# Window attention in two layers: masks and sinks laid down first in the scores' PSUM banks, one mask product per head, sinks as float32r products of three parts

## The chip, the cores and the metric

One core of one Trainium2 chip runs the whole program. The metric is the device time in microseconds of that core, from launch to end. A profiled execution has its own time, and a span from its first to its last instruction.

## The reference, cut to what matters

Two transformer blocks follow one another on 512 latent tokens and 256 context tokens of width 1024. The first block has full attention (a low-rank kind and a grouped kind), an mLSTM mixer and two feed-forward layers. The second block has two layers, each with windowed attention, a Fourier mixer, a short convolution and a gated merge. Only the windowed attention is changed:

```python
BLOCK = WINDOW = 128; 8 heads of 64, 2 key/value heads
def sink_softmax(s, sink_b):
    m = jnp.maximum(jnp.max(s, axis=-1, keepdims=True), sink_b)
    e = jnp.exp(s - m)
    return e / (jnp.sum(e, axis=-1, keepdims=True) + jnp.exp(sink_b - m))

# for each block of 128 latent queries (start = i * BLOCK):
valid = (jnp.abs(qpos[:, None] - kpos[None, :]) <= WINDOW) & (kpos >= 0) & (kpos < n)
s_loc = jnp.where(valid, einsum('bqkgd,bnkd->bkgqn', qi, ks), -jnp.inf)
s_ctx = einsum('bqkgd,bnkd->bkgqn', qi, kc)          # all 256 context tokens
p = sink_softmax(concatenate([s_ctx, s_loc]), sink_b)
o = p[..., :nc] @ vc + p[..., nc:] @ vs
# context queries (layer 0 alone): the 256 context keys, the same sink softmax
```

A block of 128 latent queries sees the context (two tiles of 128 keys), its own tile, and its left and right neighbour where there is one; the neighbours are masked along a diagonal.

## The kernel before, in words

Everything is laid out with features on partitions. Five engine programs are written out by hand; each engine runs its own list in order, and waits are semaphores with named steps (`step("s", w, p, s)` and the like). `plan()` lists the phases; here the phases `("attn", "win0")` and `("attn", "win1")` matter, each between the layer's projection jobs and its Fourier mixer.

`attn_pairs` lists the pairs of a stage. A pair is one tile of 128 queries (`qt`) and two heads, `s` = 0 and 1, one of each key/value head. Layer 0 has 24 pairs (two context tiles, four latent tiles, times four `j`), layer 1 has 16. A pair has `L` columns of scores: 256 for a context tile, 512 for the first and the last latent tile, 640 for the two in the middle. One more column, at `L`, holds the sink, so `wide` is `L + 1`. Head `s` writes its scores in the two PSUM banks `pairs[s]`.

On TensorE, `scores(p)` waits until the exponentials of pair `p - 1` have been read out of both heads' banks. For each piece of columns it issues one float32 product per head, head 0 in the upper 64 rows of the array and head 1 in the lower 64 (a float32 product is two instructions in the trace). Pieces are cut at column 512 and at the edges of masked tiles. Behind a piece with a masked tile it adds the mask by a float32r product of the identity with the mask (`BAND`), one for each masked tile and head; at the end comes a float32 product of one row of ones and the sink. Step `("s", w, p, s, 0)` is given when 512 columns are complete, `("s", w, p, s)` after the sink. Then `turn(u)` transposes the previous pair's probabilities, and `pv` multiplies them by the values, one half of a block of two pairs behind each pair.

On VectorE, `negmax` takes the maximum of the first 512 columns, then of the rest (the sink among it), and combines them; `evict` copies a quarter of the transposes; `scale` divides by the sum. On ScalarE, `exps` takes the exponential of `wide` columns with its sum, and `evict` copies the other three quarters. The order on ScalarE is: the previous pair's first eviction, both exponentials, the two other evictions. On VectorE it is: both heads' maxima, one eviction, both scalings.

Before the first scores of a stage, VectorE writes `BAND` (identity and two masks, two casts, lines 1812 and 1813) and TensorE waits for step `("band", w)`. These casts stand in VectorE's list behind its last product of the projection jobs (`Y`, line 1633). `BAND` lies in the space of the scratch row `T[5]`.

In the trace a score product is line 1069, a mask line 1073, a sink line 1077, a transpose line 1120, a value product line 1133; VectorE's maxima are lines 1821 and 1823 (line 1828 for 256 columns), the combination line 1825 (1830), its eviction 1839, its scaling 1846 and 1848; ScalarE's exponential is line 1448 and its eviction 1458.

Of the kernel before, what the change touches and what calls it, by code (L numbers as in the profile page):

```python
# [16 lines left out]
F32 = mybir.dt.float32  # L17
# [273 lines left out]
def build_program(nc, dram, step):  # L291
# [73 lines left out]
    BAND = sb("BAND", [P, 3, P], 188, F32R)  # L365
# [49 lines left out]
    def attn_pairs(which):  # L415

        pairs_of = []

        def pair(**kw):
            kw["b"], kw["r"] = len(pairs_of) // 2, len(pairs_of) % 2  # L420
            kw["nt"] = kw["L"] // P
            kw["wide"] = kw["L"] + (kw["sink"] is not None)
            pairs_of.append(kw)

        if which == "even":
            for hp in range(HEADS // 2):
                for qt in range(6):
                    L = CTX if qt < 2 else TOK
                    pair(q=[MQ[:, 2 * hp + s, qt * P:qt * P + P] for s in range(2)], L=L, masks=[], sink=None, split=False,
                         k=[(0, [MK[:, 2 * hp + s, 0:L] for s in range(2)])], out=(hp, qt),  # L430
                         v=[[VM[:, i, (2 * hp + s) * 64:(2 * hp + s) * 64 + 64] for i in range(L // P)] for s in range(2)])
            for qt in range(6):
                L = CTX if qt < 2 else TOK
                for j in range(4):
                    pair(q=[GQ[64 * s:64 * s + 64, j, qt * P:qt * P + P] for s in range(2)], L=L, masks=[], sink=None, split=True,
                         k=[(0, [GK[64 * s:64 * s + 64, 0, 0:L] for s in range(2)])], out=(j, qt),
                         v=[[VG[:, i, 64 * s:64 * s + 64] for i in range(L // P)] for s in range(2)])
        else:
            l = int(which[3])
            t0 = 0 if l == 0 else CTX  # L440
            for qt in range(t0 // P, 6):
                near = [i for i in (qt - 1, qt, qt + 1) if 2 <= i < 6] if qt >= 2 else []
                masks = [(CTX + n * P, 1 if i < qt else 2) for n, i in enumerate(near) if i != qt]
                tiles = [0, 1] + near
                ks = [(0, [SK[64 * s:64 * s + 64, 0, 0:CTX] for s in range(2)])]
                if near:
                    ks.append((CTX, [SK[64 * s:64 * s + 64, 0, near[0] * P:near[-1] * P + P] for s in range(2)]))
                for j in range(4):
                    c = PARAMS["sink"] + l * HEADS + j
                    sinks = [PAR[0:1, c + 4 * s:c + 4 * s + 1] for s in range(2)]  # L450
                    pair(q=[SQT[64 * s:64 * s + 64, j, qt * P - t0:qt * P - t0 + P] for s in range(2)], k=ks, L=len(tiles) * P,
                         masks=masks, sink=sinks, split=True, out=(j, qt),
                         v=[[SV[:, i, 64 * s:64 * s + 64] for i in tiles] for s in range(2)])
        return pairs_of
# [456 lines left out]
    def _(eng):  # L911
# [73 lines left out]
        for p in phases:  # L985
# [59 lines left out]
            elif p[0] == "attn":  # L1045
# [9 lines left out]
                def scores(p):  # L1055
                    x = prs[p]
                    pieces = []
                    for c0, k in x["k"]:
                        n = k[0].shape[-1]

                        edges = {512 - c0} | {e - c0 for m in x["masks"] for e in (m[0], m[0] + P)}
                        cuts = sorted(c for c in edges if 0 < c < n)
                        for a, b in zip([0] + cuts, cuts + [n]):
                            pieces.append((c0 + a, c0 + b, [t[:, a:b] for t in k]))
                    last = [None, None]

                    def piece(s, a, b, k, ms):
                        pos = (64 * s, 0) if x["split"] else (0, 0)
                        last[s] = mm(pairs[s][:, a:b], x["q"][s], k[s], start=True, stop=not ms, tile_position=pos)  # L1069

                    def mask(s, ms):
                        for c, m in ms:
                            last[s] = mm(pairs[s][:, c:c + P], BAND[:, 0, :], BAND[:, m, :], start=False, stop=True)

                    def sink(s):
                        if x["sink"] is not None:
                            last[s] = mm(pairs[s][:, x["L"]:x["wide"]], ONES[0:1, :], x["sink"][s], start=True, stop=True)
# [9 lines left out]
                    if x["split"]:  # L1087
                        free_scores(0)
                        free_scores(1)
                        for a, b, k in pieces:  # L1090
                            ms = [m for m in x["masks"] if a <= m[0] < b]
                            piece(0, a, b, k, ms)
                            piece(1, a, b, k, ms)
                            for s in range(2):
                                mask(s, ms)
                                if x["wide"] > 512:
                                    first_bank(s, b)
                        for s in range(2):
                            sink(s)
                            last[s].then_inc(*pe.mark("s", w, p, s))  # L1100
                    else:
                        for s in range(2):
                            free_scores(s)
                            for a, b, k in pieces:
                                piece(s, a, b, k, [])
# [434 lines left out]
    def _(eng):  # L1540
# [169 lines left out]
        for pi, p in enumerate(phases):  # L1710
# [429 lines left out]
```

## Time and profile before

| | us |
|---|---|
| median of 3 runs | 2902.92 |
| lowest and highest | 2902.10, 2913.47 |
| the profiled execution | 2902.85 |
| its span, first to last instruction | 2901.0 |
| TensorE busy (products) | 2635.5 |
| VectorE busy | 1297.1 |
| ScalarE busy | 932.1 |
| mean granted TensorE clock | 0.946 of full |

The busy times are over the whole program; the ends of products are modelled, so a busy TensorE is not one at its peak. A granted clock of 1.00 is 2.4 GHz, 0.50 is 1.2 GHz. The window attention stages lie at 2330 to 2443 us (layer 0) and 2725 to 2817 us (layer 1) of the span.

### The profile page before, as it was taken

What the parts mean: (1) busy time and instruction counts of PE and PEld (TensorE: products, weight loads), DVE (VectorE), ACT (ScalarE), POOL (GpSimd) and SP (SyncE); (2) the same over time, 40 slices, a digit from 0 to 9 for tenths busy, and PEclk for the clock granted to TensorE, in tenths of its full rate; (3) what the DMA queues carried; (4) which work ended last, traced back from release to release, by engine and by line L of the source; (5) the groups of instructions that cost most, each with busy time, mean ns of one, the idle gap of its engine ahead of it and who ended that gap; (6) DMA issues with size and microseconds to landing.
All of it is one profiled execution on the core that took longest, in us unless ns stands there. A gap on an engine that the chain in (4) does not pass through costs nothing.

```text
span 2901.0 us, 35381 instructions
## 1 busy us (share of the span) xinstructions
PE 2635.5 (91%) x14496; PEld 2032.7 (70%) x14496; DVE 1297.1 (45%) x2324; ACT 932.1 (32%) x1619; POOL 173.3 (6%) x134
## 2 busy tenths in 40 slices
PE   4988799997999999989998989999979989949997
PEld 2765555585888888867876667777858866828765
DVE  3235378835333333354435453334452264373463
ACT  3234355623212122234233332222332143332342
POOL 0000001001101011010000010101100001000010
PEclk9999889997999999998999899999979999969898
DMA  5123300011343332211120135553211210102201
GB/s 213 64 70 92 119 13 1 1 44 59 114 132 110 123 118 68 68 55 59 59 73 1 30 121 169 167 171 127 88 55 62 60 54 1 54 23 84 98 1 58
DMA packets 66001, 223.20 MB, mean 77 GB/s; under 512 B 7216, under 2 KB 10928, under 8 KB 65072
## 3 DMA queue, kind: packets, MB, share of 16 engines
q1 hardware_dynamic: 63648, 214.13, 22.9%
q10 hardware_dynamic: 2192, 6.82, 0.6%
q8 instruction: 114, 1.87, 0.3%
q14 instruction: 47, 0.39, 0.0%
HBM read 218.82 MB, written 2.10 MB: 76 GB/s over the span
## 4 chain that ended last, share of the span: by engine, by line
PE 82%; DVE 10%; ACT 4%; DMA 2%; issue 1%; POOL 0%; SPq 0%; DVEq 0%; ACTq 0%
PE pair L959 21%; PE pair L961 20%; PE pair L960 20%; PE pair L1069 4%; DVE T L1790 3%; PE side L934 2%; PE side L1133 2%; PE pair L982 2%; ACT T L1448 2%; PE pair L1120 1%; DMA RAW<-in_w 1%; PE pair L1002 1%; DVE HL L1782 1%; PE pair L653 1%; PE pair L652 1%
## 5 line engine op out<-in xcount | busy, mean ns | idle before, releaser
L959 PE MATMUL pair<-HH,WH 128*128 128x512 f32 (+1 forms) x2432 | 886.5, 365 | 70.2 <-DVE HL L1782 67.5
L961 PE MATMUL pair<-HH,WL 128*128 128x512 f32 (+1 forms) x2432 | 865.6, 356 | 0.0
L960 PE MATMUL pair<-HL,WH 128*128 128x512 f32 (+1 forms) x2432 | 865.3, 356 | 0.0
L959 PEld LDWEIGHTS pair<-HH,WH 128*128 128x128 f32 x2432 | 465.3, 191 | 192.8 <-DVE HL L1782 87.9
L1558 DVE TENSOR_TENSOR WL<-RAW,WH 128x1024 fp32r<-128x1024 f32 (+4 forms) x286 | 320.7, 1121 | 513.0 <-ACT WH L1224 500.4
L961 PEld LDWEIGHTS pair<-HH,WL 128*128 128x128 f32 x2432 | 466.6, 192 | 65.8
L960 PEld LDWEIGHTS pair<-HL,WH 128*128 128x128 f32 x2432 | 467.3, 192 | 62.1 <-issue 2.6
L1224 ACT CAST WH<-RAW 128x1024 fp32r<-128x1024 f32 (+4 forms) x286 | 270.3, 945 | 548.9 <-DMA RAW<-in_w 531.6
L959 PE MATMUL pair<-DH,WH 128*128 128x512 f32 (+3 forms) x624 | 232.8, 373 | 8.4 <-POOL DL L1977 4.3
L960 PE MATMUL pair<-DL,WH 128*128 128x512 f32 (+3 forms) x624 | 223.6, 358 | 0.0
L961 PE MATMUL pair<-DH,WL 128*128 128x512 f32 (+3 forms) x624 | 223.1, 358 | 0.0
L1608 DVE SCALAR_TENSOR_TENSOR X<-pair,MOD,X 128x256 f32<-128x256 f32 (+1 forms) x120 | 79.4, 662 | 175.5 <-PE pair L961 172.6
L959 PEld LDWEIGHTS pair<-DH,WH 128*128 128x128 f32 (+1 forms) x624 | 119.8, 192 | 44.0 <-issue 9.9
L1448 ACT ACTIVATE T<-pair,STAT 128x768 f32<-128x768 f32 (+4 forms) x176 | 126.7, 726 | 18.6 <-DVE STAT L1830 12.0
L960 PEld LDWEIGHTS pair<-DL,WH 128*128 128x128 f32 (+1 forms) x624 | 119.7, 192 | 17.7
L961 PEld LDWEIGHTS pair<-DH,WL 128*128 128x128 f32 (+1 forms) x624 | 119.3, 191 | 18.2
L1572 DVE SCALAR_TENSOR_TENSOR T<-pair,PAR,T 128x255 f32<-128x255 f32 (+1 forms) x78 | 51.5, 661 | 170.4 <-ACT T L1283 144.4
L982 PE MATMUL pair<-T,CONST 96*96 96x512 f32 (+3 forms) x112 | 56.0, 632 | 73.1 <-DVE T L1652 45.3
L934 PE MATMUL side<-RAW,CVP 128*32 128x256 f32 x1152 | 96.9, 419 | 27.1 <-DVE CVP L1566 20.3
L1821 DVE TENSOR_REDUCE STAT<-pair 128x1 f32<-128x512 f32 x128 | 87.8, 686 | 49.5 <-PE pair L1069 38.3
L1283 ACT ACTIVATE T<-pair,PAR 128x768 f32<-128x768 f32 (+1 forms) x44 | 39.0, 886 | 191.2 <-PE pair L961 191.2
L1120 PE MATMUL pair<-CONST,T 128*128 128x128 f32 x506 | 92.8, 293 | 4.5 <-DVE T L1848 1.6
(278 smaller groups left out, 2754.1 us busy)
## 6 DMA issues: line engine op xcount, KB each, us to landing
RAW<-in_w SPq DMA_DIRECT2D x345, 512.0 KB, 3.6
RAW<-in_w SPq DMA_DIRECT2D x49, 384.0 KB, 3.1
RAW<-in_w SPq DMA_DIRECT2D x16, 256.0 KB, 2.7
DFL<-in_dft_lat ACTq DMA_DIRECT2D x4, 1024.0 KB, 7.7
X<-in_x SPq DMA_DIRECT2D x1, 3072.0 KB, 16.4
out_x<-X SPq DMA_DIRECT2D x8, 256.0 KB, 2.0
RAW<-in_w SPq DMA_DIRECT2D x12, 128.0 KB, 2.0
RAW<-in_w SPq DMA_DIRECT2D x8, 144.0 KB, 2.1
```

The costliest lines, as they stand in the source:

```text
L934: ins = mm(strip, CVP[:, round * 4 + k, :], RAW[:, s, k * j.m:(k + 1) * j.m], start=round == 0, stop=round == 1, tile_position=(0, 32 * k))
L959: mm(out[0:j.m, c:e], wh[k], a, start=k == 0, stop=False)
L960: mm(out[0:j.m, c:e], wh[k], b, start=False, stop=False)
L961: ins = mm(out[0:j.m, c:e], wl[k], a, start=False, stop=k == j.k - 1)
L982: ins = mm(pairs[2][0:rows, c:e], ones[0:rows, 0:rows], sq[0:rows, c:e], start=True, stop=True)
L1069: last[s] = mm(pairs[s][:, a:b], x["q"][s], k[s], start=True, stop=not ms, tile_position=pos)
L1120: ins = nc.tensor.transpose(attn_turned(c)[:, (i - a) * P:(i - a) * P + P], T[2 * (p % 2) + s][:, i * P:i * P + P], IDENT)
L1224: nc.scalar.copy(WH[:, j.n % NRING, 0:c], RAW[:, j.n % NRING, 0:c]).then_inc(*act.mark("hi", j.n))
L1448: A(T[2 * (p % 2) + s][:, 0:x["wide"]], pairs[s][:, 0:x["wide"]], AF.Exp, bias=STAT[:, st + 2 + s:st + 3 + s], accum_out=STAT[:, st + 6 + ...
L1558: TT(WL[:, j.n % NRING, 0:c], RAW[:, j.n % NRING, 0:c], WH[:, j.n % NRING, 0:c].bitcast(F32), ALU.subtract).then_inc(*dve.mark("lo", j.n))
L1790: STT(t[:, a:b], X[:, k, t0 + a:t0 + b], AB[:, s, k:k + 1], T[3][:, a:b], ALU.mult, ALU.mult).then_inc(*dve.mark("nmul", q["id"], k))
L1821: V.tensor_reduce(m[0], pairs[s][:, 0:512], AX, ALU.max).then_inc(*dve.mark())
```

## The change

- The score columns are reordered: the masked neighbours stand first, side by side, then the two context tiles, then the query's own tile. The neighbours of a middle tile are not adjacent in the keys, so one product reads both with a stride. The values' tiles follow the same order.
- One mask product per head covers both neighbours (256 columns for the middle tiles, 128 for the first and last latent tile) and is issued as the first product of the bank; the scores accumulate on it. The pieces are no longer cut at mask edges: three pieces for 640 columns instead of four, three for 512 columns as before.
- The sink is a float32r product of two columns with the full 128 rows, issued right after the mask, before the scores. Its operands are a matrix of ones and a matrix `SINKR[:, 3]`, whose rows 0, 1 and 2 hold the sink's three float32r parts and whose other rows are zero. It writes columns `L` and `L + 1`; only `L` is read.
- For 512 columns the step after the sink is the same as the step of the first 512 columns, for both heads.
- The two heads' score products follow each other with no mask between them.
- VectorE prepares the ones and the three parts in ten more operations before the first scores of each stage.

```diff
-    BAND = sb("BAND", [P, 3, P], 188, F32R)
+    BAND = sb("BAND", [P, 4, P], 188, F32R)
+    SINKR = sb("SINKR", [P, 4, 2 * HEADS + 2], 190, F32R)
+    SINKF = sb("SINKF", [P, 4, 2 * HEADS + 2], 190.5)
...
-                near = [i for i in (qt - 1, qt, qt + 1) if 2 <= i < 6] if qt >= 2 else []
-                masks = [(CTX + n * P, 1 if i < qt else 2) for n, i in enumerate(near) if i != qt]
-                tiles = [0, 1] + near
-                ks = [(0, [SK[64 * s:64 * s + 64, 0, 0:CTX] for s in range(2)])]
-                if near:
-                    ks.append((CTX, [SK[64 * s:64 * s + 64, 0, near[0] * P:near[-1] * P + P] for s in range(2)]))
+                beside = [i for i in (qt - 1, qt + 1) if 2 <= i < 6] if qt >= 2 else []
+                own = [qt] if qt >= 2 else []
+                tiles = beside + [0, 1] + own
+                n = len(beside) * P
+                ks, mask = [], None
+                if own:
+                    first = [1 if i < qt else 2 for i in beside]
+                    mask = BAND[:, first[0]:first[-1] + 1, :]
+                    ks.append((0, n, [SK[64 * s:64 * s + 64, 0, beside[0] * P:beside[-1] * P + P].rearrange("p (t x) -> p t x", x=P)[:, 0::2, :] for s in range(2)]))
+                ks.append((n, CTX, [SK[64 * s:64 * s + 64, 0, 0:CTX] for s in range(2)]))
+                if own:
+                    ks.append((n + CTX, P, [SK[64 * s:64 * s + 64, 0, qt * P:qt * P + P] for s in range(2)]))
...
-                        for a, b, k in pieces:
-                            ms = [m for m in x["masks"] if a <= m[0] < b]
-                            piece(0, a, b, k, ms)
-                            piece(1, a, b, k, ms)
+                        for s in range(2):
+                            if x["mask"] is not None:
+                                mm(pairs[s][:, 0:pieces[0][1]], BAND[:, 0, :], x["mask"], start=True, stop=False)
+                            if x["sink"] is not None:
+                                mm(pairs[s][:, x["L"]:x["L"] + 2], BAND[:, 3, :], x["sink"][s], start=True, stop=True)
+                        for n, (a, b, k) in enumerate(pieces):
                             for s in range(2):
-                                mask(s, ms)
+                                piece(s, a, b, k, n == 0 and x["mask"] is not None)
                                 if x["wide"] > 512:
                                     first_bank(s, b)
+                                    if x["L"] == 512:
+                                        pe.also("s", w, p, s)
                         for s in range(2):
-                            sink(s)
-                            last[s].then_inc(*pe.mark("s", w, p, s))
+                            if b > 512 or x["wide"] <= 512:
+                                last[s].then_inc(*pe.mark("s", w, p, s))
...
                     V.tensor_copy(BAND[:, 0, :], IDENT).then_inc(*dve.mark())
-                    V.tensor_copy(BAND[:, 1:3, :], CONST[:, 5:7, :]).then_inc(*dve.mark("band", w))
+                    V.tensor_copy(BAND[:, 1:3, :], CONST[:, 5:7, :]).then_inc(*dve.mark())
+                    V.tensor_copy(BAND[:, 3, :], ONES).then_inc(*dve.mark())
+                    c = PARAMS["sink"]
+                    left = PAR[:, c:c + 2 * HEADS]
+                    for n in range(2):
+                        V.tensor_copy(SINKR[:, n, 0:2 * HEADS], left).then_inc(*dve.mark())
+                        dve.wait_ge(*dve.own())
+                        TT(SINKF[:, n, 0:2 * HEADS], left, SINKR[:, n, 0:2 * HEADS].bitcast(F32), ALU.subtract).then_inc(*dve.mark())
+                        left = SINKF[:, n, 0:2 * HEADS]
+                        if n == 0:
+                            TS(SINKF[:, 2, 0:2 * HEADS], SINKR[:, 0, 0:2 * HEADS].bitcast(F32), IDENT[:, 0:1], None, ALU.mult).then_inc(*dve.mark())
+                        dve.wait_ge(*dve.own())
+                    STT(SINKF[:, 3, 0:2 * HEADS], SINKR[:, 1, 0:2 * HEADS].bitcast(F32), IDENT[:, 1:2], SINKF[:, 2, 0:2 * HEADS], ALU.mult, ALU.add).then_inc(*dve.mark())
+                    dve.wait_ge(*dve.own())
+                    V.memset(SINKF[:, 3, 2 * HEADS:2 * HEADS + 2], 0.0).then_inc(*dve.mark())
+                    STT(SINKR[:, 3, 0:2 * HEADS], SINKF[:, 1, 0:2 * HEADS], IDENT[:, 2:3], SINKF[:, 3, 0:2 * HEADS], ALU.mult, ALU.add).then_inc(*dve.mark())
+                    dve.wait_ge(*dve.own())
+                    V.tensor_copy(SINKR[:, 3, 2 * HEADS:2 * HEADS + 2], SINKF[:, 3, 2 * HEADS:2 * HEADS + 2]).then_inc(*dve.mark("band", w))
```

The first block's attention calls the same `scores` with no mask and no sink; its instructions stay the same.

## Rows read from the trace of the kernel before

**Rows 1.** The page, part 4: the chain that ended last, by engine.

```profile
PE 82%; DVE 10%; ACT 4%; DMA 2%; issue 1%; POOL 0%; SPq 0%; DVEq 0%; ACTq 0%
```

**Rows 2.** Windows: from:to, length, busy us of each engine, granted clock, DMA.

```profile
2332.70:2346.40 13.70, 12.39 (x45) 7.25 (x45) 7.29 (x30) 4.68 (x23) 0.00 (x0) 0.50 0.44 183
2348.67:2357.44 8.77, 7.86 (x48) 4.47 (x49) 7.20 (x30) 4.76 (x23) 0.00 (x0) 1.00 0.00 0
2357.44:2374.72 17.28, 15.46 (x121) 11.24 (x121) 13.72 (x47) 8.67 (x29) 0.00 (x0) 1.00 0.01 2
2374.72:2419.34 44.62, 43.36 (x349) 31.97 (x347) 33.08 (x94) 21.45 (x58) 0.00 (x0) 1.00 0.00 1
2419.34:2433.59 14.25, 14.06 (x110) 9.99 (x109) 10.30 (x34) 7.17 (x22) 0.00 (x0) 1.00 0.01 1
2725.30:2749.10 23.80, 20.66 (x101) 17.12 (x100) 14.13 (x43) 8.38 (x25) 0.00 (x0) 0.50 0.35 132
```

**Rows 3.** The chain in time, two pairs of 640 columns: start, us, engine and line.

```profile
2385.59 0.92 PE pair L1069 x8
2386.51 0.37 PE pair L1073 x2
2386.88 0.65 PE pair L1069 x8
...
2387.89 0.53 PE pair L1077 x4
...
2388.94 0.49 ACT PTW L1458
...
2391.13 0.92 PE pair L1069 x8
...
2395.46 1.45 PE side L1133 x12
```

**Rows 4.** The timeline of the first of these pairs, VectorE and ScalarE.

```profile
2387.33 0.69 DVE L1821 TENSOR_REDUCE STAT<-pair 128x1 f32<-128x512 f32 x1 [1.10 <-PE pair L1069]
2388.24 0.29 DVE L1823 TENSOR_REDUCE STAT<-pair 128x1 f32<-128x129 f32 x1 [0.21 <-PE pair L1077]
...
2388.70 0.68 DVE L1821 TENSOR_REDUCE STAT<-pair 128x1 f32<-128x512 f32 x1
2389.30 0.28 DVE L1823 TENSOR_REDUCE STAT<-pair 128x1 f32<-128x129 f32 x1
...
2389.61 0.21 DVE L1825 TENSOR_SCALAR STAT<-STAT 128x1 f32<-128x1 f32 x1
...
2390.10 0.80 ACT L1448 ACTIVATE T<-pair,STAT 128x641 f32<-128x641 f32 x1
```

**Rows 5.** The timeline of VectorE, pairs of 512 columns (first tile, last tile).

```profile
2367.52 0.69 DVE L1821 TENSOR_REDUCE STAT<-pair 128x1 f32<-128x512 f32 x1 [0.87 <-PE pair L1073]
...
2369.04 0.15 DVE L1823 TENSOR_REDUCE STAT<-pair 128x1 f32<-128x1 f32 x1
2369.22 0.21 DVE L1825 TENSOR_SCALAR STAT<-STAT 128x1 f32<-128x1 f32 x1
...
2425.82 0.69 DVE L1821 TENSOR_REDUCE STAT<-pair 128x1 f32<-128x512 f32 x1 [0.84 <-PE pair L1069]
```

**Rows 6.** The chain in time, the scores of the same two pairs.

```profile
2366.08 1.15 PE pair L1069 x12
...
2424.09 0.90 PE pair L1069 x8
```

**Rows 7.** The timeline of VectorE, its last cast before the stage in layer 0.

```profile
2329.59 0.29 DVE L1813 CAST BAND<-CONST 128x256 fp32r<-128x256 f32 x1
```

**Rows 8.** Windows in the first block's grouped attention, columns as in rows 2.

```profile
480.50:503.20 22.70, 18.05 (x118) 9.20 (x116) 19.04 (x63) 13.32 (x51) 10.48 (x8) 1.00 0.00 1
503.20:510.00 6.80, 6.36 (x21) 2.75 (x21) 4.13 (x14) 2.52 (x12) 0.00 (x0) 0.50 0.00 0
518.90:585.00 66.10, 62.70 (x433) 38.54 (x435) 60.26 (x158) 45.19 (x103) 0.00 (x0) 1.00 0.00 1
```

More of the change, by code:

```diff
@@ L428, in attn_pairs @@
                     L = CTX if qt < 2 else TOK
-                    pair(q=[MQ[:, 2 * hp + s, qt * P:qt * P + P] for s in range(2)], L=L, masks=[], sink=None, split=False,
-                         k=[(0, [MK[:, 2 * hp + s, 0:L] for s in range(2)])], out=(hp, qt),
+                    pair(q=[MQ[:, 2 * hp + s, qt * P:qt * P + P] for s in range(2)], L=L, mask=None, sink=None, split=False,
+                         k=[(0, L, [MK[:, 2 * hp + s, 0:L] for s in range(2)])], out=(hp, qt),
                          v=[[VM[:, i, (2 * hp + s) * 64:(2 * hp + s) * 64 + 64] for i in range(L // P)] for s in range(2)])
@@ L434, in attn_pairs @@
                 for j in range(4):
-                    pair(q=[GQ[64 * s:64 * s + 64, j, qt * P:qt * P + P] for s in range(2)], L=L, masks=[], sink=None, split=True,
-                         k=[(0, [GK[64 * s:64 * s + 64, 0, 0:L] for s in range(2)])], out=(j, qt),
+                    pair(q=[GQ[64 * s:64 * s + 64, j, qt * P:qt * P + P] for s in range(2)], L=L, mask=None, sink=None, split=True,
+                         k=[(0, L, [GK[64 * s:64 * s + 64, 0, 0:L] for s in range(2)])], out=(j, qt),
                          v=[[VG[:, i, 64 * s:64 * s + 64] for i in range(L // P)] for s in range(2)])
@@ L441, in attn_pairs @@
             for qt in range(t0 // P, 6):
[L442 to L447 removed]
+                beside = [i for i in (qt - 1, qt + 1) if 2 <= i < 6] if qt >= 2 else []
[10 more added lines that the diff above has]
+                    ks.append((n + CTX, P, [SK[64 * s:64 * s + 64, 0, qt * P:qt * P + P] for s in range(2)]))
                 for j in range(4):
[L449 to L450 removed]
+                    c = l * HEADS + j
+                    sinks = [SINKR[:, 3, c + 4 * s:c + 4 * s + 2] for s in range(2)]
                     pair(q=[SQT[64 * s:64 * s + 64, j, qt * P - t0:qt * P - t0 + P] for s in range(2)], k=ks, L=len(tiles) * P,
[L452 removed]
+                         mask=mask, sink=sinks, split=True, out=(j, qt),
                          v=[[SV[:, i, 64 * s:64 * s + 64] for i in tiles] for s in range(2)])
@@ L1057, in scores, with piece @@
                     pieces = []
[L1058 to L1064, printed above, removed]
+                    for c0, n, k in x["k"]:
+                        for a, b in ((c0, min(512, c0 + n)), (max(512, c0), c0 + n)):
+                            if a < b:
+                                whole = b - a == n
+                                pieces.append((a, b, k if whole else [t[:, a - c0:b - c0] for t in k]))
                     last = [None, None]
-                    def piece(s, a, b, k, ms):
+                    def piece(s, a, b, k, masked):
                         pos = (64 * s, 0) if x["split"] else (0, 0)
[L1069 to L1077, printed above, removed]
+                        last[s] = mm(pairs[s][:, a:b], x["q"][s], k[s], start=not masked, stop=True, tile_position=pos)
                     def first_bank(s, b):
```

2 lines of the change are left out of this document (1 added, 1 removed).

## The prediction

> **What bounds the kernel now.** I read the page first for its shares and its chain of waits: the chain that ended last lies 82% on TensorE and 10% on VectorE [rows 1], so a product taken out of the chain can shorten the kernel. The change touches only the two window attention stages. Their stretches are in [rows 2]; one pair of heads is a period there, and a period repeats within 0.02 us. In the first layer: eight pairs of 256 columns (three of them 8.77 us), four pairs of 512 columns for the first latent query tile (17.28 us, 4.32 each), eight periods of 640 columns (44.62 us), then 14.25 us for three periods of 512 columns of the last tile (4.75 each). The second layer has no 256 columns, spends 23.80 us at a granted clock of 0.50 (1.2 GHz) on its first pairs, and then repeats the 44.62 and the 14.25 us. In the first layer the 0.50 lasted 13.70 us.
>
> The chain in a pair of 640 columns [rows 3] is: scores and masks 0.92 + 0.37 + 0.65 + 0.37 us, sinks 0.53, transposes, ScalarE's eviction at 3.35 (2388.94 - 2385.59), exponentials, and the next scores at 5.54 (2391.13). So on the face of it TensorE's scores set the period. The queue order says why: ScalarE's exponentials of the next pair stand behind the eviction of this one, which waits for TensorE's transposes, which stand behind the scores. But VectorE's maxima run beside it [rows 4]: first maximum at 1.74 after the first product, second at 2.65 (it waited 0.21 us for the sink), head 1's first at 3.11, its second 0.60 later, its last small operation at 4.02, done with its release at 4.26. ScalarE began head 1's exponential at 4.51. VectorE's path is only 0.25 us behind the bound. That is the number on which the forecast turns.
>
> **The change, part by part.**
>
> (a) *TensorE's group in a pair of 640 columns.* Before: 0.92 + 0.37 + 0.65 + 0.37 + 0.53 = 2.84 us for 24 products. After: per head one mask of 256 columns and one sink lead, then 12 instead of 16 score products. The trace has no such leading block. The two first products are priced as the mask pair with its switch back to half-height products, 0.37 [rows 3], the two others as sink steps of 0.11 (four sinks with a switch behind them took 0.53), so 0.59. Bounds: 0.44 if all four are 0.11, 0.74 if they are twice 0.37. The scores: 512 columns took 1.15 us in one run of products [rows 6], four products of 128 columns add 0.22 (the 0.65 holds eight of them and a switch near 0.2), so 1.37. Sum 1.96, a saving of 0.88 us in each of 16 pairs. In those of the pairs that hold twelve value products (1.45 us, [rows 3]) TensorE itself was the bound, with a period of 5.71; there it drops out as well.
>
> (b) *What is late next.* The first maximum needs 512 columns of scores, now behind the whole leading block: 0.59 + 1.15 = 1.74, where it was 1.74. It does not come earlier at all. What goes is the wait for the sink: second maximum at 1.74 + 0.60 = 2.34, head 1's first 0.46 later at 2.80, its second 3.40, the last small operation 3.71, released 0.24 later at 3.95 (steps from [rows 4]). ScalarE's path would allow 4.51 - 0.88 = 3.63, so VectorE is the bound. From head 1's exponential to the next scores it is 5.54 - 4.51 = 1.03, so the period becomes 4.98. The TensorE path of a pair with twelve value products: 1.96, the same eviction, transposes and value products as before less 0.88, 5.78 - 0.88 = 4.90, just under it. So 16 x 4.98 = 79.7 against 2 x 44.62 = 89.2: **-9.5 us**.
>
> (c) *512 columns, first latent tile.* Here the mask stood last and the first maximum could start at 1.44 (2367.52 - 2366.08, [rows 5, 6]). After, it waits for the leading block: 0.59 + 1.15 + 0.04 = 1.78. VectorE was already the path there: head 1's second maximum, of one column, began at 2.96, its small operation 0.18 later [rows 5], released 0.24 later at 3.38, without a wait behind the first maximum. So everything moves by the difference, +0.31 to 0.34, and TensorE's 0.33 us that are saved behind it gain nothing. Four pairs in layer 0: **+1.3 us**.
>
> (d) *512 columns, last tile.* The mask stood in the middle, the first maximum at 1.73 (2425.82 - 2424.09, [rows 5, 6]), now 1.76 to 1.78. The period becomes that of (c), 4.64; three were 14.25, now 13.92; two layers: **-0.7 us**.
>
> (e) *256 columns.* Two sinks lead instead of four that follow; 0.37 + the same four products; the maxima waited before for the first sink, now for the scores. Within 0.05 each, +0.2 for all eight. The second layer's three slow pairs of 512 columns: the leading block costs VectorE about 0.6 at the half clock, TensorE saves about as much; the pair with value products, which TensorE binds, gains 0.5. **-0.2 us** for (e) together.
>
> (f) *The preparation on VectorE.* Ten operations more: one of 128 columns, nine of 2 to 16, in front of TensorE's first scores, which wait for the last of them. Nothing hides it: TensorE stood idle since its last product and VectorE had only just ended its product for Y. Before, the second cast's row lasted 0.29 [rows 7]. A small dependent step is 0.18 (2369.22 - 2369.04, [rows 5]); seven such, 0.14 for the 128 columns, two near 0.1 that wait for nothing, and 0.06: 1.6 us. Bounds: ten times 0.07 and ten times 0.21 (the small operation's own duration, [rows 4]), so 0.7 to 2.1. Two layers: **+3.2 us**. The initial wait of ScalarE's first exponential moves with it; its four transfers of Fourier tables are issued before and needed only after the stage.
>
> (g) *Clock.* Taken as unchanged, 0.
>
> Sum: -9.5 + 1.3 - 0.7 - 0.2 + 3.2 = -5.9 us. The profiled execution took 2902.85 us (span 2901.0 and 1.85 around it), which is 0.07 from the median of 2902.92. The stage ends go through to the kernel's end, since the Fourier products follow on the same engine. Forecast **2897.0 us**.
>
> **A rule of the Trainium skill against it.** The row first: in the first block's grouped attention, TensorE was busy for 18.05 of 22.70 us in pairs of 256 columns, and then the granted clock was 0.50 for the next 6.8 us; in pairs of 768 columns it was busy 62.70 of 66.10 and the clock stayed at 1.00 [rows 8]. The Trainium skill, "TensorE: Matmul & The Clock Gate", section "A second HAM failure mode: psum-queue depth-cycling", says that an engine which pauses briefly but often between groups of matmuls swings between its two clocks. By that rule the thinner groups after the change would cost time; the trace agrees for 256 columns and disagrees for 768. What it would cost here is worked out from rows in C and D.
>
> **The rivals.**
>
> *A. The forecast* (VectorE's maxima become the path). For it: 4.26 against 4.51 today. Chance 0.57; by its own bounds (leading block +-0.15 on some 30 pairs is +-4.5, preparation -1.8 to +1.0) 2891 to 2903.
>
> *B. TensorE's saving counts in full*, because the first maximum comes earlier than worked out (the leading products' weights load while TensorE waits for the exponentials). 16 x 0.88 = 14.1, for 12 pairs of 512 columns about 0.4 each, 4.8, less 3.2: 2887. Against it: the leading block must then cost VectorE nothing. Chance 0.06.
>
> *C. The clock is regained late.* Both stages begin at 0.50, and the first layer returns to 1.00 in pairs of 256 columns, which lose four of sixteen products. If it stays down to the pairs of 512 columns, two pairs of 512 columns lose about 2.3 each (23.80 us held some three and a half periods of the second layer, 6.7 each, against 4.32; [rows 2]) and four of half the columns about half of that: +9, so 2906. For it: [rows 8]. Against it: in the second layer the first pairs with value products brought it back. Chance 0.18.
>
> *D. The other side: the clock falls in the pairs of 640 columns.* TensorE's 1.96 + 0.5 before ScalarE's eviction would double, +2.4 on each; all 16: +38, so 2935. With nine pairs or more it is slower than before by over 0.5%, and from three pairs on no longer faster. Against it: after the change TensorE works about 4.4 to 4.9 of 4.98 us there, near the 0.95 of the pairs of 768 columns. Chance 0.05.
>
> *E. The change hardly acts*: another path (ScalarE's exponentials, VectorE's scaling of head 1) takes over at once, or the leading block is 0.74 and more. The period goes to 5.3 only: -4 in (b), +1.3 + 3.2: 2903. Chance 0.14.
>
> **How the numbers follow.** The likeliest is A, 2897.0. A change of 0.5% is 14.5 us, about what a measurement of this kernel can tell from none: one of the three runs of before lay at 2913.47. The range holds A, C and E and leaves B and D out: 2889 to 2908. Faster by over 0.5% (below 2888.4) needs B: 0.05. Slower by over 0.5% (above 2917.4) needs D or a later clock in both stages: 0.05. The rest, 0.90, is within 0.5%.
>
> **What would show it.** Pairs of 640 columns at a period of 4.98 with the first maximum still near 1.74 and its successor no longer waiting; the chain there through VectorE's maxima; the first latent tile's pairs at 4.6 instead of 4.32; 1.6 us more between VectorE's product for Y and TensorE's first scores; recorded score products down from 480 to 416 (a float32 product is two records), sinks from 160 to 80, masks from 96 to 64. Wrong would be: a first maximum that moves by more than 0.15, a clock of 0.50 inside the 640 columns, or a leading block far from 0.59.

## The result and the profile after

The changed kernel takes 2887.23 us (median of 18 runs, 2883.76 to 2895.39), the kernel before 2902.43 in the same comparison (18 runs, 2891.37 to 2913.99). The ratio is 0.9947, 95% interval 0.9934 to 0.9959: 15.2 us less, between 12 and 19. The forecast was 2897.0, some 6 less, in a range of 2889 to 2908. So the direction was right, and the size was not: the time lies 1.8 us below the range.

The profiled execution of after took 2895.39 us, the slowest of its 18, so its distance to the profile of before (2902.85) is 7.5 us. One execution is not the median here, and much of what follows is about that. (Over all profiled executions of the study the five of before have a mean of 2900.8 us and the three of after 2894.6, 6.2 less.)

Windows of after, to be laid beside [rows 2] (from:to, length, busy TensorE, weight loads, VectorE, ScalarE, GpSimd, granted clock, DMA):

```profile
2372.17:2381.29 9.12, 7.39 (x61) 5.22 (x61) 6.95 (x24) 4.98 (x15) 0.00 (x0) 1.00 0.00 1
2381.29:2420.72 39.43, 35.87 (x282) 25.81 (x283) 31.24 (x93) 22.85 (x57) 0.00 (x0) 1.00 0.01 1
2420.72:2434.40 13.68, 12.38 (x102) 8.78 (x103) 10.33 (x35) 7.80 (x22) 0.00 (x0) 1.00 0.01 1
2727.23:2747.83 20.60, 14.34 (x97) 11.65 (x97) 12.47 (x42) 8.63 (x24) 0.00 (x0) 0.75 0.34 132
2747.83:2787.27 39.44, 35.87 (x282) 25.79 (x283) 31.23 (x93) 22.85 (x57) 0.00 (x0) 1.00 0.01 1
```

The first row holds two pairs of the first latent tile, 4.56 each where it was 4.32. The second and the last hold the eight periods of 640 columns, 39.43 and 39.44 us where it was 44.62: 4.93 each, where they were 5.33 to 5.71. The third holds three periods of the last tile, 13.68 where it was 14.25. The fourth is the start of layer 1 up to the 640 columns, at a mean clock of 0.75.

The chain in a pair of 640 columns after (start, us, engine and line), beside [rows 3]:

```profile
2391.15 0.36 PE pair L1090
2391.50 0.00 PE pair L1092
2391.51 0.22 PE pair L1090
2391.73 0.00 PE pair L1092
2391.73 1.11 PE pair L1075 x8
2392.85 0.67 DVE STAT L1840
2393.52 0.21 DVE STAT L1842
2393.73 0.03 issue
2393.76 0.21 DVE STAT L1844
2393.97 0.60 DVE STAT L1840
```

Line 1090 is the mask, 1092 the sink, 1075 a score product. The masks lead; eight score products later the chain leaves TensorE for VectorE's maxima and stays there. Before, it went on through masks, sinks, transposes and ScalarE's eviction.

VectorE and ScalarE in the same pair, beside [rows 4]:

```profile
2392.83 0.69 DVE L1840 TENSOR_REDUCE STAT<-pair 128x1 f32<-128x512 f32 x1 [1.04 <-PE pair L1075]
2393.44 0.28 DVE L1842 TENSOR_REDUCE STAT<-pair 128x1 f32<-128x129 f32 x1
...
2394.80 0.21 DVE L1844 TENSOR_SCALAR STAT<-STAT 128x1 f32<-128x1 f32 x1
...
2395.05 0.80 ACT L1450 ACTIVATE T<-pair,STAT 128x641 f32<-128x641 f32 x1 [0.16 <-DVE STAT L1844]
```

The first maximum begins 1.68 us after the first product (before 1.74), the second follows without a wait, and ScalarE's second exponential waits 0.16 us for VectorE's last small operation. Forecast for these were 1.74, no wait, and VectorE as the bound.

The preparation in layer 0, its first two rows and its last, and the first product behind it, beside [rows 7]:

```profile
2332.99 0.22 DVE L1814 CAST BAND<-CONST 128x128 fp32r<-128x128 f32 x1
2333.13 0.28 DVE L1815 CAST BAND<-CONST 128x256 fp32r<-128x256 f32 x1
...
2334.98 0.17 DVE L1832 CAST SINKR<-SINKF 128x2 fp32r<-128x2 f32 x1
...
2335.30 0.35 PE L1092 MATMUL pair<-SINKR,BAND 128*128 128x2 f32 x2 [4.07 <-DVE SINKR L1832]
```

From the first cast (2332.99) to the first product it is now 2.31 us. Before it was 0.57:

```profile
2329.45 0.22 DVE L1812 CAST BAND<-CONST 128x128 fp32r<-128x128 f32 x1
...
2330.02 0.70 PE L1069 MATMUL pair<-SK,SQT 64*128 64x256 f32 x4 [2.32 <-DVE BAND L1813]
```

The recorded instructions are those that were foretold: 416 score products for 480, 80 sinks for 160, 64 masks for 96.

What the profile does not bear out is the size of the whole. The same window over both stages, from the first cast to the first Fourier product, gives for before and for after:

```profile
2329.45:2443.00 113.55, 105.08 (x752) 72.46 (x753) 80.23 (x262) 53.36 (x169) 0.00 (x0) 0.94 0.08 30
2724.27:2817.72 93.45, 87.62 (x624) 65.06 (x624) 62.42 (x186) 41.11 (x113) 0.00 (x0) 0.87 0.10 37
```

```profile
2332.99:2443.75 110.76, 93.67 (x656) 62.53 (x656) 79.93 (x272) 57.08 (x169) 0.00 (x0) 0.91 0.08 31
2724.91:2810.30 85.39, 70.74 (x545) 51.35 (x545) 61.01 (x196) 43.91 (x113) 0.00 (x0) 0.94 0.11 40
```

Together 207.00 before and 196.15 after, 10.9 less. Between the stages lie 281.3 and 281.2 us and behind them 83.3 and 83.3, the same. But the first stage begins at 2329.45 before and at 2332.99 after: 3.5 us more went by in the same code ahead of the change. And the mean clock went from 0.87 to 0.94 in layer 1 and from 0.94 to 0.91 in layer 0. The time at 1.2 GHz follows from the mean, 2 x (1 - mean) x length: 14 and 24 us before, 20 and 10 after. The slow stretch does not start with the stage: in before it began 2.7 us after the first product in layer 0 and 0.4 in layer 1.

### The profile page after: what moved, and what is told of

It reads as the page before. It is cut to its first block, busy times and chain, and to the rows that moved or that the text cites. A ratio compares the mean times of both kernels' runs of the same rounds, so it can differ in the third digit from the quotient of the medians.

```text
span 2893.6 us, 35049 instructions
## 1 busy us (share of the span) xinstructions
PE 2610.2 (90%) x14320; PEld 2010.8 (69%) x14320; DVE 1295.2 (45%) x2344; ACT 938.6 (32%) x1619; POOL 173.3 (6%) x134
## 4 chain that ended last, share of the span: by engine, by line
PE 80%; DVE 12%; ACT 4%; DMA 2%; issue 1%; POOL 0%; SPq 0%; DVEq 0%; ACTq 0%
PE pair L967 21%; PE pair L969 20%; PE pair L968 20%; PE pair L1075 4%; DVE T L1792 3%; PE side L942 2%; PE pair L990 2%; DVE STAT L1840 2%; PE side L1135 2%; ACT T L1450 2%; DMA RAW<-in_w 1%; PE pair L1122 1%; PE pair L1010 1%; PE pair L661 1%; PE pair L660 1%
```

## The experiments

Three questions: is the steady part what the periods say, how much is the clock, and which part of the change carries which.

**1. Both kernels once more.** No edit.

> The changed kernel once more, for a second profile. Theory P (the pairs): in the steady stretches the change is worth a fixed amount, 640 columns at a period of 4.93 us instead of 5.58 on the mean, first latent tile 4.56 instead of 4.32, last tile 4.56 instead of 4.75, preparation +1.74 us a layer, together about -7.3 us, and every profile repeats these to 0.02. Theory C (the clock): what is beyond -7.3 in the median of -15.2 comes from stretches at a granted clock of 0.50, which differ from one execution to the next; then this profile shows other such stretches than the first one, and its sum of them explains its time. Rival U (upstream): the change moves something outside the window stages; then a stretch outside them is shorter in this profile than before at an equal clock.

> The kernel before once more, for a second profile and as a measure of how far two equal kernels differ: ratio 1.000 within 0.003. Theory P: periods 5.54 and 5.71, 4.32, 4.75 repeat. Theory C: the first pairs of layer 1 stay at 0.50 for 14 to 31 us, the length differs from the first profile's 23.9. Rival U: the stretches outside the stages are as in the first profile.

Measured: *again* 2891.43 us beside 2906.43, ratio 0.9948 (0.9929 to 0.9967); *before_again* ratio 0.9997 (0.9981 to 1.0013). The periods at a clock of 1.00 repeated to 0.02 us. The stages of *again* took 114.39 + 85.94 = 200.33 us:

```profile
2326.19:2440.58 114.39, 99.25 (x656) 64.78 (x657) 80.05 (x272) 56.98 (x169) 0.00 (x0) 0.85 0.08 30
2721.75:2807.69 85.94, 71.73 (x545) 52.08 (x545) 61.02 (x196) 43.92 (x113) 0.00 (x0) 0.92 0.11 40
```

Against the first profile of after that is 4.2 us more with the same instructions, and the mean clock in layer 0 is 0.85 instead of 0.91. *before_again* had 113.54 + 93.46, as the first, and the same 14 and 24 us at 1.2 GHz; I had expected layer 1's to differ. So theory C holds for after, and this profile of before shows nothing of it. Between and behind the stages nothing changed (281.2 and 83.3 us), so rival U fell for these parts. Ahead of them it can't be settled from profiles: the first stage began at 2323.6 (before) and 2326.2 (after) here, and over all 18 profiles of this study it began anywhere from 2318.6 to 2333.8. Their code up to there is the same, but for nine small operations at the start of four of them and the products added just ahead of the stage in the five *hold* kernels.

**2. The two halves of the change.** *masks_only* takes out of the changed kernel the leading sinks and their preparation:

```diff
-    mm(pairs[s][:, x["L"]:x["L"] + 2], BAND[:, 3, :], x["sink"][s], start=True, stop=True)
...
+    last[s] = mm(pairs[s][:, x["L"]:x["wide"]], ONES[0:1, :], x["sink"][s], start=True, stop=True)
```

*sinks_only* gives the kernel before the leading float32r sinks, in place of its own, and the preparation, and keeps its pieces and masks.

> The new column order and the one leading mask per head, but the sinks as before: a float32 product of one row, last, and no preparation on VectorE. Theory P: the leading block is 0.37 instead of 0.53, so the first maximum comes at about 1.52 in a pair of 640, and TensorE's group is 0.37 + 1.37 + 0.53 = 2.27; ScalarE's path and VectorE's are about level, period 4.95; first latent tile 4.40 instead of 4.56; no preparation. So about -10 us against before, 2 to 4 us below the changed kernel. If instead the sinks' new form carries the gain, this one is near before (-3 or less).

> The columns, pieces and masks as before; only the sinks in the new form, leading, with the preparation. Theory P: the first maximum comes 0.33 later in every pair with masks, which lengthens the first latent tile by 0.33 and the last by 0.3, while 640 columns gain 0.16 to 0.25 (no wait for the sink, TensorE's group 0.16 shorter): -2.5 to -4 + 1.4 + 2.4 + 3.5 = +3 to +5 us against before. The rival that the sinks' form carries the gain expects -5 or less.

Measured: *masks_only* 2900.07, ratio 0.9992 (0.9971 to 1.0012); *sinks_only* 2898.73, ratio 0.9974 (0.9958 to 0.9990). Both were the other way round from what I expected. Yet their steady periods came as worked out: *masks_only* had 4.99 and 5.16 us for 640 columns and 4.42 to 4.68 for the last tile, *sinks_only* 5.28 and 5.34, then 4.60 for the first tile and 4.91 for the last. What had changed beside them was the clock:

```profile
2324.01:2444.96 120.95, 115.35 (x705) 78.07 (x705) 80.33 (x262) 53.16 (x169) 0.00 (x0) 0.79 0.08 28
2726.12:2816.01 89.89, 83.95 (x576) 61.40 (x576) 61.27 (x186) 41.14 (x113) 0.00 (x0) 0.85 0.10 38
```

That is *masks_only*: 51 and 27 us at 1.2 GHz. *sinks_only* had 34 and 21. In the profiles both have longer stages than before (210.8 and 211.0 us for 207.0), while *sinks_only* is faster in the times. So one profile's stages and the median of the timed executions can differ by some 10 us, and neither half could be priced as long as the clock ran free.

**3. The clock held.** Products of constants are added on TensorE where it waits at the start of each stage. They write a bank that is written anew before it is read. *hold_after*, and later *hold_sinks*, have two more of them, where TensorE waits for the preparation.

```diff
+    def keep(n, cols=512):
+        if w != "even":
+            for _ in range(n):
+                mm(side[0][:, 0:cols], IDENT, CONST[:, 0:cols // P, :], start=True, stop=True)
+    take("side0")
+    keep(3)
     pe.wait_ge(*step("ready", w))
...
     scores(0)
+    keep(2)
...
         turn(u)
+        if u < 2:
+            keep(1 if prs[u + 1]["L"] == 256 else 3, 256)
```

> The kernel before with float32 products of constants added on TensorE (into a bank that nothing reads before it is written again) where it waits at the start of each window stage: three ahead of the stage, two after the first scores, one or three short ones behind the first two pairs' transposes. Output unchanged. Theory C: the granted clock then stays at 1.00 through both stages, layer 1's first three pairs fall from 24.6 to about 15 us and layer 0's first four from 18.7 to 14: some -10 us against before, and the pair with the changed kernel plus the same products gives the change's worth without the clock. If the clock falls all the same, the added products cost up to 2 us.

> The changed kernel with the same added products (two more ahead of the stage, where it waits for the preparation). Theory P: against hold_before it is faster by the steady amount alone, 7 to 8 us, since both keep the clock in the stages. If it is faster by 13 or more, the steady periods do not hold the whole of the change, and something else is to be found.

Measured: *hold_before* 2887.10, ratio 0.9939 (0.9926 to 0.9953); *hold_after* 2880.90, ratio 0.9922 (0.9907 to 0.9938). Their stages:

```profile
2322.69:2432.55 109.86, 103.54 (x762) 70.77 (x760) 80.07 (x262) 53.47 (x169) 0.00 (x0) 1.00 0.08 31
2713.95:2801.18 87.23, 84.68 (x644) 60.51 (x642) 61.27 (x186) 41.06 (x113) 0.00 (x0) 1.00 0.11 40
```

```profile
2322.03:2429.12 107.09, 93.21 (x670) 61.70 (x669) 79.78 (x272) 57.17 (x169) 0.00 (x0) 0.98 0.08 32
2710.16:2793.63 83.47, 75.03 (x568) 52.28 (x566) 60.99 (x196) 43.85 (x113) 0.00 (x0) 1.00 0.11 41
```

At a clock of 1.00 the change is worth 197.09 - 190.56 = 6.5 us, and 2887.10 - 2880.90 = 6.2 us in the times, where the two intervals overlap. That is the steady amount, and it is what the forecast's sum of 5.9 was about. (The clock fell once more in *hold_after*, for 3.4 us in layer 0, and cost one pair 0.9.) The surprise is the other number: holding the clock alone takes 9.9 us off the stages of the kernel before, and 17 us (14 to 21) off its time, as much as the whole change (12 to 19). It does not make the times scatter less: the six runs of *hold_before* spread over 4.4 us, but those of *hold_after* over 10.5, for 12.7 in eleven runs of the kernel before.

**4. The halves with the clock held, and one sink edit alone.** *hold_masks* and *hold_sinks* are experiment 2 with the products of 3. *sinks_last* is the kernel before with only this, the parts made at the start:

```diff
-    last[s] = mm(pairs[s][:, x["L"]:x["wide"]], ONES[0:1, :], x["sink"][s], start=True, stop=True)
+    last[s] = mm(pairs[s][:, x["L"]:x["L"] + 2], BAND[:, 3, :], x["sink"][s], start=True, stop=True)
```

> The new masks and order with the old sinks, and the added products that hold the clock. Theory S (steady part and clock part are separate, and the old one-row float32 sinks go with the clock part): with the clock held this is 9 to 11 us below hold_before and 3 to 5 below hold_after, as its periods of about 5.0 and 4.4 us and its missing preparation say, although without the added products the same kernel was level with before. Rival: the masks alone are worth 2 us at any clock.

> The old masks with the new sinks, and the added products. Theory S: with the clock held this is 2 to 5 us above hold_before (periods 5.28 instead of 5.58, but 4.60 and 4.91 instead of 4.32 and 4.75, and 3.5 for the preparation), although without them it was 7.5 us below before. Rival: the new sinks are worth 7 us at any clock.

> The kernel before with one thing changed: the sink is the float32r product of two columns on 128 rows, in its old place behind the scores, its parts made at the program's start; no products added. Steady part by the periods: TensorE's group 0.25 shorter, 640 columns at 5.35, the 512 columns unchanged: -4 to -5. Theory S: the clock part of the one-row float32 sinks goes as well, -6 to -10 more: 2889 to 2894 beside 2904. Rival L, that the clock part needs the sinks or masks to lead: -5 alone.

Measured: *hold_masks* 2883.47, ratio 0.9924 (0.9904 to 0.9944), stages 105.01 + 81.77 = 186.78 us; *hold_sinks* 2889.13, ratio 0.9949 (0.9932 to 0.9966), stages 111.79 + 88.04 = 199.83; *sinks_last* 2895.04, ratio 0.9968 (0.9953 to 0.9984), stages 202.46.

```profile
2330.26:2435.27 105.01, 98.25 (x714) 66.11 (x712) 79.29 (x262) 53.89 (x169) 0.00 (x0) 1.00 0.09 33
2718.03:2799.80 81.77, 78.99 (x596) 56.18 (x595) 60.49 (x186) 41.40 (x113) 0.00 (x0) 1.00 0.12 42
```

By the stages, with the clock held, the masks alone are worth 197.09 - 186.78 = 10.3 us and the sinks alone cost 2.7 (1.1 of it in one pair, where the clock fell for 3.4 us); both together give 6.5. So in the steady part the new sinks with their preparation are a loss, of 3.8 us on top of the masks. The preparation alone is 3.5, and the short fall of the clock in *hold_after* 0.9, so the leading sinks themselves about break even. In the times, which carry the scatter of the code ahead of the stages, *hold_masks* lies only 3.6 us below *hold_before*, from another comparison, and its six runs spread over 12; I take the stages here, and the times don't confirm the 10.3. *sinks_last* had periods of 5.10 and 5.28 us for 640 columns (I expected 5.35), and 4.62 in all pairs of the last tile, so some 7 of its 9 us are steady. It had 58 us at 1.2 GHz in its stages, more than four of the five profiles of the kernel before. Nothing here shows that the form of the sinks shortens the slow stretches, as theory S had it.

What the form does change is the price of a slow stretch. The stages' excess over the held twin, by the time at 1.2 GHz: *masks_only* 24.1 us for 78, before 9.9 for 38 (and 16.7 for 58, below); *sinks_only* 11.2 for 55, after 5.6 for 31 and 9.8 for 48; *sinks_behind* (experiments 5 and 6) 11.5 for 51. With the old sinks 0.26 to 0.31 us are lost for each us at 1.2 GHz, with the new ones 0.18 to 0.23.

The rows show it. A pair of 256 columns at 1.2 GHz before, and one after:

```profile
2336.89 1.23 PE pair L1069 x4
2338.11 0.94 PE pair L1077 x4
```

```profile
2345.43 0.56 PE pair L1092 x2
2345.99 1.15 PE pair L1075 x4
```

Four one-row float32 sinks took 0.94 us; the two new ones take 0.56 up to the first score product. Pairs of 256 columns have no mask, so they show the sinks alone. Once value products follow, TensorE has no pause in such a pair at 1.2 GHz, and its period there is 4.39 to 4.40 us in every profile with the old sinks (before, *masks_only*), 3.97 with the new ones ahead of the scores (after, *sinks_only*) and 3.90 with them behind. At 1.00 it is 2.92, 2.90 and 2.82.

With 512 columns, a pair of layer 1 without value products and wholly at 1.2 GHz took 6.16 us before and 5.90 in *prep_early*, which has the same products as after. Masks and sinks had taken 0.62 + 0.94 = 1.56 us of TensorE's time in it, behind the scores; in *prep_early* they took 0.99, in front. TensorE saved 0.57, but VectorE's maxima waited for what now stood in front, and the chain of the new pair went through them. The fourth pair has value products: it took 7.14 us before, all of it on TensorE. No profile shows it wholly at 1.2 GHz with the new masks and sinks; in *prep_early* it took 5.90, but there its value products already ran at the full clock (1.08 us for eight, 1.75 before).

**5. The steps of the forecast, one by one.** *prep_early* makes the sinks' parts once, at the program's start, and keeps only the three casts of `BAND` at a stage. *sinks_behind* is that with the float32r sinks issued after the scores.

> The changed kernel, with the nine small operations of the sinks' parts made once at the program's start, where VectorE waits, and only the cast of the ones left before each stage. Theory P: TensorE's first scores come 1.5 us sooner behind the product for Y in each stage, -3.0 us against the changed kernel, if the clock's stretches are the same. Rival: the small operations were hidden and it makes no difference.

> As prep_early, and the sinks (float32r, two columns) issued after the scores instead of ahead of them. Theory that VectorE's path binds from the first maximum on: the first maximum comes 0.22 sooner, periods 4.93 to 4.71 (16 pairs), 4.56 to 4.34 (12 warm pairs), -6 us against prep_early. Rival, that ScalarE's path through TensorE's transposes binds: no change or +0.1 a pair, since TensorE's group stays as long or a switch longer.

Measured: *prep_early* 2891.48, ratio 0.9957 (0.9942 to 0.9973); *sinks_behind* 2886.64, ratio 0.9943 (0.9927 to 0.9958). In *prep_early* the first product comes 0.70 us after the first cast, where it was 2.31, so 1.6 us a layer came off. In the time a gain of 3 us is below what its interval can tell, and none is seen. Nor is one in the stages, 110.35 + 85.42 = 195.77 us for 196.1: the condition of equal stretches was not met, with 41 us at 1.2 GHz for 31. In *sinks_behind* the first maximum begins at 1.57 (2386.67 - 2385.10) and the period of 640 columns is 4.82 to 4.87, that of the last tile 4.39 to 4.42. I expected 4.71 and 4.34. Its stages were 111.71 + 81.64 = 193.35 us, 51 of them at 1.2 GHz. The chain says what stopped it:

```profile
2385.10 0.47 PE pair L1090 x2
2385.57 1.29 PE pair L1075 x12
2386.86 0.31 PE pair L1098 x2
2387.17 0.42 PE pair L1119 x3
2387.59 0.02 issue
2387.61 0.49 ACT PTW L1457
```

The path through the sinks (1098), transposes (1119) and ScalarE's eviction is back. So VectorE's maxima bind in the changed kernel, and 0.1 us behind them stands the old bound.

**6. The version that these point to.** *sinks_behind* with the products that hold the clock.

> The version that the runs point to: new masks leading, sinks as float32r behind the scores, their parts made at the start, and the added products. Stages by the periods of sinks_behind without its stretches at 0.50: 640 columns 4.85, 512 columns 4.40, 256 columns 2.85 to 2.90: 3 to 5 us below hold_after, 2876 to 2878 beside 2904 for the kernel before, ratio 0.9905.

Measured: 2878.56 us beside 2903.93, ratio 0.9907 (0.9887 to 0.9927), stages 102.03 + 79.79 = 181.82 us. It is the fastest of the study by its stages, 8.7 us below *hold_after* where I expected 3 to 5; by the times the two cannot be told apart.

**7. More profiles.** No edits.

> The kernel before, a third profile. Its two window stages took 207.0 us together in both profiles so far, 9.9 over those of hold_before, while the medians say 17. If timed executions lose more to the clock than the two profiles show, some of the next profiles have stages of 210 to 217 us, with more than 37.6 us at 0.50 in them; if it is always 207.0, the missing 8 us lie elsewhere.

> The kernel before, a fourth profile: stages of 207.0 us again, or of 210 to 217 with more at 0.50, as in the third.

> The kernel before, a fifth profile: stages of 207.0 us again, or of 210 to 217 with more at 0.50, as in the third.

> The changed kernel, a third profile: stages of 196 to 200 us together, 31 to 48 us of them at 0.50, as in its two profiles so far.

Measured, the stages together: 207.03, 207.01 and 213.83 us for before, 196.09 for after. The fifth profile of before was the one with more at 1.2 GHz, 38 us in layer 0 and 21 in layer 1:

```profile
2322.50:2443.68 121.18, 114.81 (x752) 78.07 (x752) 80.70 (x262) 53.01 (x169) 0.00 (x0) 0.85 0.08 29
2724.85:2817.50 92.65, 86.45 (x624) 64.02 (x624) 62.31 (x186) 41.11 (x113) 0.00 (x0) 0.89 0.10 37
```

So the stages take 207.0 four times and 213.8 once before (mean 208.4), and 196.1 twice and 200.3 once after (mean 197.5): 10.9 us less. With this the profiles locate 10.9 of the 15.2 us: 6.5 as in the pair with the clock held, and 4.3 by which the slow stretches cost less after the change (7.0 us on the mean for 11.3).

## Why the prediction was right and wrong, point by point

- (a) The leading block took 0.51 us instead of 0.59 (2391.66 - 2391.15), TensorE's group 1.80 instead of 1.96 (2392.95 - 2391.15). Within the bounds, and the saving a little larger, 1.04 for 0.88.

```profile
2391.15 0.36 PE L1090 MATMUL pair<-BAND 128*128 128x256 f32 x1 [0.54 <-ACT T L1450]
2391.34 0.17 PE L1092 MATMUL pair<-SINKR,BAND 128*128 128x2 f32 x1
2391.37 0.36 PE L1090 MATMUL pair<-BAND 128*128 128x256 f32 x1
2391.57 0.17 PE L1092 MATMUL pair<-SINKR,BAND 128*128 128x2 f32 x1
2391.66 1.36 PE L1075 MATMUL pair<-SK,SQT 64*128 64x256 f32 x12
2392.95 0.55 PE L1122 MATMUL pair<-CONST,T 128*128 128x128 f32 x3
```

- (b) Right in mechanism and size. The bound moved to VectorE's maxima; the period is 4.93 for 4.98, the 16 periods gave -10.4 us for -9.5. Rival B fell here: the first maximum came 0.06 earlier, no more. Its 2887 us is nevertheless the time that was measured (2887.23); that is chance, since its 14.1 us of full saving in the pairs of 640 columns were 10.4. E and D fell too: the clock was 1.00 in all pairs of 640 columns of the three profiles of after.
- (c) Right: the first latent tile became slower, 4.56 us at a clock of 1.00 (forecast 4.64), +1.0 us for +1.3.
- (d) Right: 13.68 us (forecast 13.92), -1.1 us for -0.7.
- (f) 1.74 us a layer for 1.6; it is exposed, as *prep_early*'s 0.70 to the first product shows.
- Sum of the steady part: the clock-held pair measured -6.5 and -6.2 for a forecast of -5.9.
- (e) At a clock of 1.00 right: 2.90 us for 2.92 in a pair of 256 columns. At 1.2 GHz I took what TensorE saves and what the leading block costs VectorE as equal, and only the pair with value products as a gain, of 0.5. Layer 1's second pair gained 0.25 instead, and layer 0's pairs of 256 columns with value products, for which the forecast had nothing at this clock, gain 0.42 each. (Its own terms, +0.2 and -0.5, make -0.3, not -0.2.) What is far larger is not in (e) at all: the start of layer 1 went from 24.6 us (2724.84 to 2749.45) to 20.60, 4.0 less, but most of that is the third pair, 6.16 and then 4.56 us, because the clock was back at 1.00, and the value products of the fourth, for the same reason.
- (g) **This step failed:** "Clock. Taken as unchanged, 0." The slow stretches in the two stages cost 9.9 to 16.7 us before and 5.6 to 9.8 after, on the mean 11.3 and 7.0: the term was worth -4.3 us, not 0 (with what (e) has at 1.2 GHz). It is the sum of two things, fewer us at 1.2 GHz (38 to 58 before, 31 to 48 after) and a lower price of each. Rival C had the clock as a cost of the change. In layer 0 the stretch was longer in all three profiles of after (20, 34 and 20 us for 14 in four of five, 38 in the fifth), as C says; in layer 1 it became shorter (10, 14, 10 for 24, 24, 24, 24 and 21). None of the signs of being wrong that the prediction names came up: they look at the first maximum, at the leading block and at the clock inside the 640 columns, and not at the clock at the start of a stage.
- Of the 9.3 us that the forecast missed, then, 0.6 lie in the steady part, 4.3 in the clock, and 4.4 in nothing that a profile shows.
- The rule cited from the Trainium skill ("TensorE: Matmul & The Clock Gate", section "A second HAM failure mode: psum-queue depth-cycling"), of TensorE swinging between its clocks when it often pauses, was not borne out in the pairs of 640 columns, with 35.87 us busy of 39.43 at 1.00. In the thinner pairs ahead of them the trace agrees with it: in two of three profiles of after the clock came back in layer 0 and fell once more, which no stage of the five profiles of before did.

```profile
2353.50:2367.10 13.60, 10.51 (x70) 6.15 (x70) 10.36 (x40) 7.27 (x28) 0.00 (x0) 1.00 0.00 0
2367.10:2370.60 3.50, 3.50 (x21) 3.07 (x21) 1.75 (x6) 0.65 (x2) 0.00 (x0) 0.51 0.02 5
```

Open: the profiles of the stages give 10.9 us, the comparison of the times 12 to 19 and 10 to 21 in its repetition. The same gap stands in *hold_before*, 9.9 to 16.7 us by the stages and 17 by the times. So timed executions of the kernel before may lose more at 1.2 GHz than four of its five profiles show; the fifth is of that kind. How often they do was not measured, and the scatter ahead of the stages, 15 us over the profiles, may hold a part as well. What makes the stretch in layer 1 shorter was not settled either. The five profiles of kernels with both the new masks and the new sinks (after three times, *prep_early*, *sinks_behind*) have 10 to 17 us there, the eight others with a free clock 21 to 27, either half of the change alone among them. So it seems to take both halves, though most of these kernels have one profile each; by what path they act, no run isolates.

## What to carry to other kernels

When a product is taken out of a path, write down the path that runs beside it and its distance: here 0.25 us, and the 1.04 us that TensorE saved in a pair of 640 columns became 0.65 in the period. Moving masks and sinks ahead of the scores was no gain for VectorE, which waits for the first complete bank (its first maximum came 0.06 us sooner); it took away only the wait behind that bank. And before pricing microseconds in a kernel that starts its stages with a pause of TensorE, hold the clock there with work nobody needs: it was worth about as much as the change, and without it neither half of the change could be read.

## What the runs showed of the hardware

- A float32r product of two columns behind one of 256 columns delayed the next product by 0.03 us: the mask started at 2391.15, the sink at 2391.34 and the next mask at 2391.37. The step from the mask to the sink was 0.19.
- Float32 products added in TensorE's pauses (some 5 us of work in layer 0 and 7 in layer 1) kept the granted clock at 1.00 through both stages of *hold_before*, where the kernel before was at 0.50 for 38 to 58 us. Its stages are 9.9 to 16.7 us shorter for it and its time 17. In *hold_after* and *hold_sinks* the clock still fell once, for 3.4 us.
- A pair of 256 columns with value products, on which TensorE has no pause at 1.2 GHz, took 4.39 us there and 2.92 at 2.4 GHz with four one-row float32 sinks, 3.97 and 2.90 with two float32r sinks of two columns.
- The five profiles of the same program (before) began their first window stage within 7 us of each other (2322.5 to 2329.5), the 18 of kernels with nearly the same code up to there within 15 (2318.6 to 2333.8). The time at 0.50 ahead of it, by an estimate from windows of 10 us between 201 and 267 us, does not go with the start: 256 us in *hold_before* and 201 in *hold_after*, which began at 2322.7 and 2322.0.
